# Building the in-pair table of an S5 scan during the scan itself, from a table turned back on TensorE, instead of in the front of the kernel

## The chip, the cores and the metric

The kernel runs on one NeuronCore of a Trainium2 chip. A core has TensorE (PE, with its weight loads listed apart as PEld), VectorE (DVE), ScalarE (ACT), GpSimd (POOL) and SyncE (SP), which here only issues DMA transfers. The metric is the device time of one execution in microseconds. The kernel before takes 2447.58 us (median of 3 runs, 2445.82 to 2447.65). The execution that the profiler recorded took 2450.09 us, with a span of 2448.3 us.

## What is computed

The program is a trunk of two residual layers on 256 tokens of width 2048. Layer 0 mixes tokens with a diagonal complex state-space model (S5), layer 1 with sparse attention; each is followed by a SwiGLU FFN, and shift, scale and gate of every sublayer come from a conditioning vector. The change lies in the S5 mixer:

```python
u = h @ in_w                                     # 128 groups of 16 channels
lam_bar = jnp.exp(lam * dt)
b_bar = ((lam_bar - 1.0) / lam)[..., None] * bmat
bu = jnp.einsum('gnp,blgp->lbgn', b_bar, ug)
# states[l] = lam_bar * states[l-1] + bu[l]
_, states = lax.associative_scan(combine, (a_seq, bu), axis=0)
y = jnp.real(jnp.einsum('gpn,lbgn->blgp', cmat, states)).reshape(Bsz, L, D)
y = y + d_skip.astype(f32) * u.astype(f32)
g = jax.nn.gelu(y).astype(h.dtype)
z = g @ glu_w + glu_b
```

Each group has 64 complex states. Everything is in float32.

## The kernel before

**Pairs of tokens.** The 256 tokens are taken in 128 pairs. VectorE runs the recurrence over pairs, so a step multiplies by the square of `lam_bar` and 128 states are made, not 256. What the first token of a pair gives to a state is in the table `Btab[1]` (B times lambda), what the second gives in `Btab[0]` (B). The output of a pair's second token needs the state before the pair, through C times lambda and so on, and also a term inside the pair: its own input through C times B, plus the skip term. `K0` holds that term, one 128 x 128 tile for each of the 16 blocks `f` of 128 channels, nonzero only inside groups of 16 channels. `Ddiag` holds the skip term alone, as 16 diagonal tiles, for the first token.

**The front (0 to 68 us).** TensorE and ScalarE turn C and B into tables. `turn_diag` (L1936) transposes `Bdiag` (B spread to block-diagonal form) into `Btab[0]`, four tiles at a time, with ScalarE copying the bank out (L868). `in_pair` (L1946) then multiplies `Bdiag` by `Ctab[0]`, 8 matmuls of 128 x 128 x 128 for each of 4 banks (L1952); VectorE multiplies each bank by a 0/1 mask into `K0` (`masked`, L1354). Later, in the first projection, VectorE adds the skip diagonal to `K0` in 16 instructions (`add_skip`, L1255). Between these, VectorE makes B times lambda in four big multiplications (`times_lam`, L1332), whose last one (L1346) must end before TensorE can transpose the imaginary half.

**Column units.** The conditioning vector is multiplied by `ada_w`, which streams from HBM in units of 512 KB through a ring of buffers `col_raw`. TensorE takes two units at a time with four matmuls (`col_units`, L1856; trace lines L1868 in the front, L1879 in the scan stage). I call that a pair of units. 64 units are consumed up to the end of the projection, and 64 more in the scan stage, through a ring of 7 buffers (`STATE_RING`): SyncE issues a unit's DMA as soon as TensorE has read the unit 7 places earlier.

**The projection (68 to 178 us)** takes 32 weight units of 512 KB, each rounded into a high part by ScalarE (L836) and a low part by VectorE (L1190), and 12 TensorE matmuls each (L2275). The other half of the column units is interleaved with its first 12.

**The scan stage (178 to 331 us).** TensorE's order is `s5()` (L2111): `inputs(0..7)` (L2058) fill the states; `outputs_inside(1, f)` and `outputs_inside(0, f)` (L2071 with `Ddiag`, L2072 with `K0`) with a pair of units after every second `f`; `outputs_inside(2, f)` with a pair after every `f`; four more pairs; then `outputs(0, f)` and `outputs(1, f)` (L2081), which need the first half of the scan, with the last nine pairs; then `outputs_inside(3)`, the first products of the GLU (L2093, L2107), `outputs(2)` and `outputs(3)`, which need the end of the scan. TensorE works strictly in that order. VectorE meanwhile runs 147 steps of the scan, six instructions each (L1531, L1536, L1542). At step 66 it reads the third row of column sums, which needs 32 of the 64 units.

## Time and profile before

| | |
|---|---|
| median of 3 runs | 2447.58 us |
| the profiled execution, and its span | 2450.09 us, 2448.3 us |
| TensorE busy, share of the span | 2395.8 us, 98% |
| VectorE, ScalarE busy | 1862.1 us (76%), 1039.9 us (42%) |
| bytes moved by DMA, mean rate | 630.53 MB, 258 GB/s |
| first matmul of the projection (L2275) | 67.68 us |
| last `inputs` matmul done, first `outputs(0)` matmul | 200.4 us, 257.1 us |
| last step of the scan | ends at 319.1 us |
| last `outputs(3)` matmul done | 331.4 us |

The profile is one execution. Times of rows count from the start of its span. A timeline or a chain of waits gives start and length in us; "x8" counts instruction records, of which an fp32 matmul leaves two. An idle time in brackets names what ended it. "PEclk" is the clock granted to TensorE, as a share of 2.4 GHz, so 1.00 and 0.50 are its two levels, 2.4 and 1.2 GHz. TensorE is busy nearly everywhere, so most of the 2448 us is its own work. The two places that the change touches are the front and the scan stage.

### The profile page before, as it was taken

How to read it: one execution, taken by the hardware profiler on the slowest of the kernel's cores; microseconds unless marked ns; L12 is line 12 of the kernel's file. 1: busy time of each engine (PE TensorE's matmuls, PEld its weight loads, DVE VectorE, ACT ScalarE, POOL GpSimd, SP SyncE). 2: the span in 40 equal slices, each digit the busy share in tenths (PEclk: the TensorE clock that was granted, in tenths of full speed). 3: DMA queues.
4: the chain of work that ended last, by engine and by line, in shares of the span. 5: the costliest groups of instructions: out<-in, count | busy, mean ns of one | idle time of the engine just before them, and what ended most of it. 6: DMA issues, size and time to landing. Idle time of an engine off the chain costs nothing.

```text
span 2448.3 us, 33308 instructions
## 1 busy us (share of the span) xinstructions
PE 2395.8 (98%) x12561; PEld 1918.2 (78%) x12561; DVE 1862.1 (76%) x3012; ACT 1039.9 (42%) x1241; POOL 35.3 (1%) x67
## 2 busy tenths in 40 slices
PE   7999899999999999999999999999999999999998
PEld 5585578778888888888878888778888888888886
DVE  8469979878888887888879987887777754455457
ACT  4353133464434444344454434555444344443442
POOL 0000000000000000000000000000000000000000
PEclk9997999999999999999999999999999999999999
DMA  9977959779889997898758877646788666656674
GB/s 373 399 256 278 373 169 328 234 236 349 306 284 308 342 308 259 292 339 297 256 162 291 284 254 226 201 141 192 253 300 279 220 196 189 189 190 191 194 223 139
DMA packets 313335, 630.53 MB, mean 258 GB/s; under 512 B 26740, under 2 KB 27156, under 8 KB 313176
## 3 DMA queue, kind: packets, MB, share of 16 engines
q1 hardware_dynamic: 307664, 613.36, 74.2%
q0 software_dynamic: 4288, 13.90, 2.0%
q8 instruction: 101, 1.65, 0.3%
q10 hardware_dynamic: 1224, 1.14, 0.1%
q14 instruction: 58, 0.48, 0.1%
HBM read 626.20 MB, written 2.11 MB: 257 GB/s over the span
## 4 chain that ended last, share of the span: by engine, by line
PE 90%; DVE 5%; issue 2%; DMA 2%; ACT 1%; SPq 0%; DVEq 0%; ACTq 0%
PE psB L2275 39%; PE psA L2275 39%; PE psT L1836 1%; PE psM L1868 1%; DMA col_raw<-in_ada_w 1%; PE psM L1879 1%; PE psB L2093 1%; DVE ada_acc L1207 1%; DVE w_lo L1190 1%; PE psT L2081 1%; PE psM L2107 1%; PE psT L2275 0%; PE psT L1900 0%; PE psA L2081 0%; PE psA L2058 0%
## 5 line engine op out<-in xcount | busy, mean ns | idle before, releaser
L1190 DVE TENSOR_TENSOR w_lo<-w_raw,w_hi 128x1024 fp32r<-128x1024 f32 x728 | 887.8, 1223 | 460.0 <-ACT w_hi L836 455.4
L836 ACT ACTIVATE w_hi<-w_raw 128x1024 fp32r<-128x1024 f32 x728 | 770.7, 1060 | 1093.5 <-PE psB L2275 486.6
L2275 PE MATMUL psB<-w_hi,hT_hi 128*128 128x512 f32 x1040 | 407.4, 392 | 0.0
L2275 PE MATMUL psB<-w_hi,hT_lo 128*128 128x512 f32 x1040 | 404.9, 389 | 0.0
L2275 PE MATMUL psB<-w_lo,hT_hi 128*128 128x512 f32 x1040 | 404.7, 389 | 0.0
L2275 PE MATMUL psA<-w_hi,hT_hi 128*128 128x512 f32 x1008 | 397.6, 394 | 2.3 <-DVE w_lo L1190 2.0
L2275 PE MATMUL psA<-w_hi,hT_lo 128*128 128x512 f32 x1008 | 392.8, 390 | 0.0
L2275 PE MATMUL psA<-w_lo,hT_hi 128*128 128x512 f32 x1008 | 392.5, 389 | 0.0
L1207 DVE SCALAR_TENSOR_TENSOR ada_acc<-ada_raw,csil,ada_acc 128x512 f32<-128x512 f32 x465 | 347.1, 746 | 14.6 <-DVE ada_acc L1207 0.5
L2275 PEld LDWEIGHTS psB<-w_hi,hT_hi 128*128 128x128 f32 x1040 | 195.3, 188 | 46.0 <-issue 4.5
L2275 PEld LDWEIGHTS psA<-w_hi,hT_hi 128*128 128x128 f32 x1008 | 189.2, 188 | 49.1 <-issue 8.0
L2275 PEld LDWEIGHTS psB<-w_hi,hT_lo 128*128 128x128 f32 x1040 | 195.2, 188 | 40.8
L2275 PEld LDWEIGHTS psB<-w_lo,hT_hi 128*128 128x128 f32 x1040 | 195.3, 188 | 39.8
L2275 PEld LDWEIGHTS psA<-w_hi,hT_lo 128*128 128x128 f32 x1008 | 189.2, 188 | 39.9
L2275 PEld LDWEIGHTS psA<-w_lo,hT_hi 128*128 128x128 f32 x1008 | 189.4, 188 | 37.8
L2275 PE MATMUL psA<-w_hi,aT_hi 128*128 128x512 f32 x448 | 175.3, 391 | 2.7 <-DVE w_lo L1190 1.9
L2275 PE MATMUL psA<-w_hi,aT_lo 128*128 128x512 f32 x448 | 174.4, 389 | 0.0
L2275 PE MATMUL psA<-w_lo,aT_hi 128*128 128x512 f32 x448 | 174.3, 389 | 0.0
L2275 PE MATMUL psB<-w_hi,aT_hi 128*128 128x512 f32 x400 | 156.3, 391 | 1.3 <-DVE w_lo L1190 1.3
L2275 PE MATMUL psB<-w_hi,aT_lo 128*128 128x512 f32 x400 | 155.7, 389 | 0.0
L2275 PE MATMUL psB<-w_lo,aT_hi 128*128 128x512 f32 x400 | 155.6, 389 | 0.0
L2275 PEld LDWEIGHTS psA<-w_hi,aT_hi 128*128 128x128 f32 x448 | 84.1, 188 | 21.5 <-DVE w_lo L1190 2.7
(399 smaller groups left out, 2356.7 us busy)
## 6 DMA issues: line engine op xcount, KB each, us to landing
w_raw<-in_ffn_w_in SPq DMA_DIRECT2D x352, 512.0 KB, 4.5
ada_raw<-in_ada_w SPq DMA_DIRECT2D x496, 256.0 KB, 5.3
w_raw<-in_ffn_w_out SPq DMA_DIRECT2D x176, 512.0 KB, 4.7
col_raw<-in_ada_w SPq DMA_DIRECT2D x128, 512.0 KB, 7.3
w_raw<-in_dsa_in_w SPq DMA_DIRECT2D x112, 512.0 KB, 4.7
w_raw<-in_s_glu_w SPq DMA_DIRECT2D x56, 512.0 KB, 5.5
w_raw<-in_s_in_w SPq DMA_DIRECT2D x32, 512.0 KB, 8.1
w_raw<-in_dsa_out_w SPq DMA_DIRECT2D x32, 512.0 KB, 4.9
```

The source lines that it names most:

```text
L836: nc.scalar.activation(high(u), w_raw[:, u % RING], ACT.Copy).then_inc(w_hi_ready, 1)
L1190: V.tensor_tensor(low(u), w_raw[:, u % RING], high(u).bitcast(F32), ALU.subtract).then_inc(w_lo_ready, 1)
L1207: V.scalar_tensor_tensor(out=ada_sum(q), in0=ada_tile(q, k), scalar=csil[:, k:k + 1], in1=ada_sum(q), op0=ALU.mult, op1=ALU.add).then_inc( ...
L1836: ins = nc.tensor.transpose(T[:, j // 2, (j % 2) * SEQ + t * P:(j % 2) * SEQ + (t + 1) * P], src(t, j), ident[:])
L1868: ins = MM(M[row:row + 32, 0], csil[:, k:k + 1].to_broadcast([P, 32]), col_tile(a + w)[:, b * NB:(b + 1) * NB], start=k == 0, stop=k == AU ...
L1879: ins = MM(M[row:row + 32, v % 2], csil[:, k:k + 1].to_broadcast([P, 32]), col_tile(a + half)[:, b * NB:(b + 1) * NB], start=k == 0, stop= ...
L2081: ins = MM(outputs_place(n, f, d)[rows], Ctab[d][ri][:, f, rows], st[:, c0:c0 + HALF, half, g, ri, f % 8], start=False, stop=f % 4 == 3 an ...
L2093: ins = MM(gated_bank(0, t), uT[:, kt, tok], glu_raw[k][:, kk], start=kt == 0, stop=kt == KT - 1)
L2107: ins = MM(gated_bank(1, 0), uT[:, kt, 0:P], raw[:, kk], start=kt == 0, stop=kt == KT - 1)
L2275: ins = MM(PS[s][:, t, 0:r.width] if into is None else into, a_[:, kt, tok], b_[:, kk, 0:r.width], start=kt == begin and m == 0, stop=kt = ...
```

## The change

The in-pair term is no longer made in the front. `in_pair` with its 32 matmuls, `masked` and `add_skip` are gone, and so are the waits on them. GpSimd clears `K0` at the start. In the scan stage, after the last `inputs`, TensorE transposes the 32 tiles of `Btab[0]` back into state-major form (`turn_back`, 8 banks of 4 tiles), ScalarE copies each bank to `Bback` (over `Btab[1]`, no longer needed then), and TensorE multiplies `Bback` by `Ctab[0]` in 128 matmuls that write 32 x 32 blocks of one PSUM bank. Four matmuls of an identity block by `Ddiag` add the skip term, and ScalarE copies the four diagonal strips to `K0` in four instructions. Only then may `outputs_inside` start. The pairs of units are placed anew: four among the eight `turn_back`, one behind the new `in_pair`, and in the third group one after every second `f` in place of every `f`.

```diff
+        Bback = [at(f"Bback_{ri}", "aT_lo", [P, KT, P], plus=ri * 8 * K) for ri in range(2)]
...
                 elif col_slot(a)[0] == CRING:
-                    sp.wait_ge(pair_full, 4)
                     sp.wait_ge(scaled_ready, 2)
...
+            nc.gpsimd.memset(K0[:], 0.0).then_inc(pair_zeroed, 1)
...
+                for n in range(8):
+                    act.wait_ge(back_turned, n + 1)
+                    nc.scalar.activation(Bback[n // 4][:, 4 * (n % 4):4 * (n % 4) + 4, :],
+                                         PS[0][:, n % 2].rearrange("p (j m) -> p j m", m=P), ACT.Copy).then_inc(back_stored, 1)
+                act.wait_ge(pair_full, 1)
+                act.wait_ge(pair_zeroed, 1)
+                for g in range(4):
+                    rows = slice(32 * g, 32 * g + 32)
+                    nc.scalar.activation(K0[rows, :, rows], PS[0][rows, 0].rearrange("p (f m) -> p f m", m=32), ACT.Copy
+                                         ).then_inc(pair_stored, 1)
...
-            def add_skip(f):
-
-                V.scalar_tensor_tensor(out=K0[:, f], in0=ident[:], scalar=dcol[:, f:f + 1], in1=K0[:, f], op0=ALU.mult, op1=ALU.add
-                                       ).then_inc(pair_skipped, 1)
...
-            for n in range(3):
-                col_units(20 + 2 * n, 22 + 2 * n)
-                in_pair(n)
-            col_units(26, 30)
-            in_pair(3)
-            col_units(30, VUNITS)
+            col_units(20, VUNITS)
...
+            def turn_back(n):
+
+                if n >= 2:
+                    pe.wait_ge(back_stored, n - 1)
+                for k in range(4):
+                    ins = nc.tensor.transpose(PS[0][:, n % 2, k * P:(k + 1) * P], Btab[0][n // 4][:, 4 * (n % 4) + k, :], ident[:])
+                ins.then_inc(back_turned, 1)
+
+            def in_pair():
+
+                pe.wait_ge(back_stored, 8)
+                for f in range(KT):
+                    for ri in range(2):
+                        for g in range(4):
+                            rows = slice(32 * g, 32 * g + 32)
+                            MM(PS[0][rows, 0, 32 * f:32 * f + 32], Bback[ri][:, f, rows], Ctab[0][ri][:, f, rows],
+                               start=f + ri == 0, stop=False)
+                pe.wait_ge(diag_ready, 2)
+                for g in range(4):
+                    rows = slice(32 * g, 32 * g + 32)
+                    ins = MM(PS[0][rows, 0].rearrange("p (f m) -> p f m", m=32), ident[rows, rows], Ddiag[rows, :, rows],
+                             start=False, stop=True, tile_position=(32 * g, 32 * g))
+                ins.then_inc(pair_full, 1)
...
-                pe.wait_ge(diag_ready, 2)
-                pe.wait_ge(pair_skipped, KT)
+                pe.wait_ge(bu_read_act, 22)
+                for n in range(8):
+                    turn_back(n)
+                    if n % 2:
+                        units(2)
+                in_pair()
+                units(2)
+                pe.wait_ge(pair_stored, 4)
                 for half, read in ((1, 20), (0, 24)):
...
                 for f in range(8):
                     outputs_inside(2, f)
-                    units(2)
-                units(8)
+                    if f % 2:
+                        units(2)
+                units(6)
```

TensorE in the front of the kernel before, from the fifth pair of column units before the end of that stretch (`col_raw` is a ring buffer of units, `C0_0_tab` the real half of `Ctab[0]`):

```order
L1868 MATMUL psM<-col_raw2_72,csil_96 32x512 x4
L1952 MATMUL psA<-C0_0_tab_123,Bdiag_re_141 128x128
L1952 MATMUL psA<-C0_1_tab_124,Bdiag_im_142 128x128
L1952 MATMUL psA<-C0_0_tab_123,Bdiag_re_141 128x128
L1952 MATMUL psA<-C0_1_tab_124,Bdiag_im_142 128x128
```

The same place in the changed kernel, up to the first transposes of B times lambda:

```order
L1861 MATMUL psM<-col_raw_72,csil 32x512 x4
L1861 MATMUL psM<-col_raw_73,csil 32x512 x4
L1861 MATMUL psM<-col_raw_74,csil 32x512 x4
L1861 MATMUL psM<-col_raw_75,csil 32x512 x4
L1861 MATMUL psM<-col_raw_71,csil 32x512 x4
L1861 MATMUL psM<-col_raw_72,csil 32x512 x4
L1935 MATMUL psA<-ident,BLdiag_re 128x128 x4
```

The four blocks of eight matmuls between the pairs of units are gone, and the six pairs now follow one another.

TensorE in the scan stage of the kernel before, behind the last `inputs`:

```order
L2058 MATMUL psB<-uT_105,B1_1_tab_122 128x127 x2
L2071 MATMUL psT<-uT_105,Ddiag_83 128x64
L2072 MATMUL psT<-uT_105,K0_127 128x64
L2071 MATMUL psT<-uT_105,Ddiag_83 128x64
L2072 MATMUL psT<-uT_105,K0_127 128x64
L1879 MATMUL psM<-col_raw2_72,csil_96 32x512 x2
```

And in the changed kernel (L2077 are the transposes of `turn_back`, L1872 the units, L2087 the small in-pair matmuls, of which 32 such rows follow):

```order
L2034 MATMUL psB<-uT,B_1_tab 128x127 x2
L2077 MATMUL psA<-ident,B_0_tab 128x128 x8
L1872 MATMUL psM<-col_raw_72,csil 32x512 x2
L1872 MATMUL psM<-col_raw_70,csil 32x512 x2
L2077 MATMUL psA<-ident,B_0_tab 128x128 x8
L1872 MATMUL psM<-col_raw_70,csil 32x512 x4
L2077 MATMUL psA<-ident,B_1_tab 128x128 x8
L1872 MATMUL psM<-col_raw_70,csil 32x512 x2
L1872 MATMUL psM<-col_raw_71,csil 32x512 x2
L2077 MATMUL psA<-ident,B_1_tab 128x128 x8
```

```order
L2087 MATMUL psA<-C_1_tab,Bback_129 32x32 x4
L2092 MATMUL psA<-Ddiag,ident 32x512 x4
L1872 MATMUL psM<-col_raw_70,csil 32x512 x4
L2047 MATMUL psT<-uT,Ddiag 128x64
L2048 MATMUL psT<-uT,K_127 128x64
L2047 MATMUL psT<-uT,Ddiag 128x64
```

Thirty-two transposes, 128 small matmuls and 4 wide ones now stand between the last `inputs` and the first `outputs_inside`, with five pairs of units among them; the pairs behind are fewer by as many.

## Rows read from the trace of the kernel before

**Rows 1.** The page: TensorE's busy time, and its granted clock in 40 slices.

```profile
PE 2395.8 (98%) x12561; PEld 1918.2 (78%) x12561; DVE 1862.1 (76%) x3012; ACT 1039.9 (42%) x1241; POOL 35.3 (1%) x67
PEclk9997999999999999999999999999999999999999
```

**Rows 2.** Stretches: length, busy us (instructions) of each engine, PEclk, DMA share, GB/s.

```profile
10.00:60.00 50.00, 47.17 (x500) 30.50 (x501) 43.27 (x56) 26.04 (x46) 0.00 (x0) 1.00 1.03 404
60.00:116.00 56.00, 54.51 (x308) 33.23 (x307) 27.18 (x40) 22.82 (x29) 0.00 (x0) 1.00 1.03 401
209.10:236.20 27.10, 27.10 (x116) 12.61 (x120) 27.10 (x173) 0.00 (x0) 0.00 (x0) 0.50 0.92 321
283.60:331.40 47.80, 47.75 (x613) 30.53 (x614) 40.05 (x258) 5.85 (x6) 0.00 (x0) 1.00 0.55 195
```

**Rows 3.** Chain of waits in the front: start, length, what.

```profile
46.24 1.98 PE psA L1952 x16
58.01 0.99 PE psM L1868 x8
61.02 2.20 DVE BLdiag_im L1346
```

**Rows 4.** VectorE in the front, a `masked`; and all of `add_skip`, grouped.

```profile
51.23 0.69 DVE L1357 TENSOR_TENSOR K<-psB,cst 128x512 f32<-128x512 f32 x1
L1257 DVE SCALAR_TENSOR_TENSOR K<-ident,dcol,K 128x128 f32<-128x128 f32 x16 | 4.8, 344 | 0.0
```

**Rows 5.** Last pair of units of the front: its two DMAs, and their time to landing.

```profile
L630 SPq DMA_DIRECT2D col_raw<-in_ada_w x2: 327/380/432, 46.3 to 46.6; - x2
DMA to landing us min/median/max: 6.8/7.3/7.8
```

**Rows 6.** Last pair of the projection: its DMAs, landing, and (chain) its matmuls.

```profile
L630 SPq DMA_DIRECT2D col_raw<-in_ada_w x2: 328/380/431, 104.8 to 105.2; - x2
DMA to landing us min/median/max: 9.4/9.9/10.3
116.48 0.99 PE psM L1868 x8
```

**Rows 7.** ScalarE and VectorE behind the last `inputs`: scan step 20 starts.

```profile
200.50 1.12 ACT L1025 ACTIVATE st<-psA 128x512 f32<-128x512 f32 x2 [1.25 <-PE psB L2058]
202.63 0.49 DVE L1531 TENSOR_TENSOR prod<-st,lam 128x128 f32<-128x128 f32 x2 [0.64 <-ACT st L1025]
```

**Rows 8.** TensorE in the scan stage, pairs of units; the first two at full clock.

```profile
203.44 1.06 PE L1879 MATMUL psM<-col_raw,csil 128*32 128x512 f32 x8
205.47 1.06 PE L1879 MATMUL psM<-col_raw,csil 128*32 128x512 f32 x8
209.08 1.83 PE L1879 MATMUL psM<-col_raw,csil 128*32 128x512 f32 x8 [1.51 <-DMA col_raw<-in_ada_w]
216.50 1.94 PE L1879 MATMUL psM<-col_raw,csil 128*32 128x512 f32 x8
220.27 1.94 PE L1879 MATMUL psM<-col_raw,csil 128*32 128x512 f32 x8
255.54 1.78 PE L1879 MATMUL psM<-col_raw,csil 128*32 128x512 f32 x8 [0.62 <-DMA col_raw<-in_ada_w]
```

**Rows 9.** Four transposes of `turn_diag` on TensorE; a bank copied by ScalarE.

```profile
59.00 0.59 PE psA L1942 x4
40.39 0.59 ACT L868 ACTIVATE B_tab<-psB 128x512 f32<-128x512 f32 x1
```

**Rows 10.** Chain of waits at the end of the stage: `outputs(2)`, `outputs(3)`.

```profile
313.24 7.26 PE psA L2081 x226
324.13 5.88 PE psT L2081 x181
```

**Rows 11.** The column unit issued at 222.2 us: time to landing.

```profile
DMA to landing us min/median/max: 3.6/3.6/3.6
```

**Rows 12.** VectorE: the last steps of the scan.

```profile
318.84 0.31 DVE L1542 TENSOR_TENSOR st<-tmp,st 128x32 f32<-128x32 f32 x2
```

More of the change, by code:

```diff
@@ L290, in build @@
         gate_saved = sem("gate_saved")
-        pair_skipped = sem("pair_skipped")
         glub_landed, sigmoid_done = sem("glub_landed"), sem("sigmoid_done")
@@ L306, in build @@
         imag_turned, imag_stored = sem("imag_turned"), sem("imag_stored")
-        pair_full, pair_masked, c_scaled = sem("pair_full"), sem("pair_masked"), sem("c_scaled")
+        c_scaled, pair_zeroed, back_turned, back_stored = sem("c_scaled"), sem("pair_zeroed"), sem("back_turned"), sem("back_stored")
+        pair_full, pair_stored = sem("pair_full"), sem("pair_stored")
         part_free, part_added = [sem("part_free0"), sem("part_free1")], sem("part_added")
@@ L930, in _ @@
             make_h(0)
-            act.wait_ge(pair_full, 4)
             h_high(0)
@@ L1353, in _, with row_at_last @@
             vec.wait_ge(c_scaled, 2)
-            def masked(n):
-                vec.wait_ge(pair_full, n + 1)
-                V.tensor_tensor(K0[:, 4 * n:4 * n + 4], PS[n % 2][:, n // 2 % 2].rearrange("p (j m) -> p j m", m=P),
-                                cst[:, 98:98 + P].unsqueeze(1).to_broadcast([P, 4, P]), ALU.mult).then_inc(pair_masked, 1)
-            def masked_then_row(n):
-                masked(n)
+            def row_at_last(n):
                 if n == 3:
@@ L1373, in _ @@
             vec.wait_ge(bdiag_ready, 8)
-            times_lam(pairs(BLdiag[0], True), pairs(BLdiag[1], True), [pairs(b, True) for b in Bdiag], True, scaled_ready, masked_then_row)
+            times_lam(pairs(BLdiag[0], True), pairs(BLdiag[1], True), [pairs(b, True) for b in Bdiag], True, scaled_ready, row_at_last)
             vec.wait_ge(scaled_turned, 2)
@@ L1780, in _ @@
                         lo_to(n, 2, filled_to(r))
-                        if n == 2:
-                            vec.wait_ge(pair_masked, 4)
-                        if 2 <= n < 10:
-                            add_skip(2 * n - 4)
-                            add_skip(2 * n - 3)
                         if n in (14, 16):
@@ L1944, in turn_diag @@
                 ins.then_inc(full, 1)
-            def in_pair(n):
-                pe.wait_ge(b_stored, n + 5)
-                for k in range(4):
-                    f = 4 * n + k
-                    for ri in range(2):
-                        ins = MM(PS[n % 2][:, n // 2 % 2, k * P:(k + 1) * P],
-                                 Bdiag[ri][:, 4 * f:4 * f + 4].rearrange("p g a k -> p (g a k)"), Ctab[0][ri][:, f],
-                                 start=k + ri == 0, stop=k + ri == 4)
-                ins.then_inc(pair_full, 1)
             pe.wait_ge(act_prep, 3)
@@ L1982, in _ @@
                 turn_diag(n, Bdiag, bdiag_ready, 5, b_stored, b_turned)
-            for n in range(3):
-                col_units(20 + 2 * n, 22 + 2 * n)
-                in_pair(n)
-            col_units(26, 30)
-            in_pair(3)
-            col_units(30, VUNITS)
+            col_units(20, VUNITS)
             pe.wait_ge(scaled_ready, 1)
             for n in range(2):
-                turn_diag(n, BLdiag, pair_masked, 1, scaled_stored, scaled_turned)
+                turn_diag(n, BLdiag, b_stored, 5, scaled_stored, scaled_turned)
             turn_row(0, M[:, 1], front_row[:, 0])
-            turn_diag(2, BLdiag, pair_masked, 1, scaled_stored, scaled_turned)
+            turn_diag(2, BLdiag, b_stored, 5, scaled_stored, scaled_turned)
             pe.wait_ge(lam_spread, 1)
@@ L1997, in _ @@
             for n in range(4, 7):
-                turn_diag(n, BLdiag, pair_masked, 1, scaled_stored, imag_turned)
-            turn_diag(3, BLdiag, pair_masked, 1, scaled_stored, scaled_turned)
+                turn_diag(n, BLdiag, b_stored, 5, scaled_stored, imag_turned)
+            turn_diag(3, BLdiag, b_stored, 5, scaled_stored, scaled_turned)
             pe.wait_ge(cols_added, 2)
@@ L2010, in projection @@
                 r = s5_in
-                pe.wait_ge(pair_masked, 4)
                 pe.wait_ge(scaled_stored, 3)
```

## The prediction

> **What bounds the kernel now.** I read four views, in this order. The page first: TensorE is busy 98% of the span, and its granted clock is below full in one slice of forty, the one from 184 to 245 us, which is the scan stage [rows 1]. So time is won where TensorE waits or is slow, and any work added to it costs its own length unless it fills a wait. Second, the stretches [rows 2]: from 10 to 116 us the DMA engines are saturated, 404 and 401 GB/s, at a DMA share over 1. A unit of 512 KB then takes 524,288 B / 404 GB/s = 1.30 us, and a pair 2.6 us. From 209.1 to 236.2 us TensorE is busy all the time at a granted clock of 0.50 while DMA moves only 321 GB/s; from 283.6 to 331.4 us it is busy 47.75 of 47.80 us. Third, the chain of waits: in the front it runs on TensorE and VectorE [rows 3], at the end of the scan stage on TensorE through `outputs(2)` and `outputs(3)` [rows 10]. Fourth, VectorE's timeline, which ends the scan at 318.84 + 0.31 = 319.1 us [rows 12], 5.0 us before TensorE starts `outputs(3)` at 324.13 [rows 10]. The scan stage is therefore bound by TensorE's order and by the column units in it, not by the recurrence: whatever delays TensorE between 200 and 283 us shifts the end one for one, and the most that speeding it up can bring is 5.0 us, for then the recurrence is last.
>
> **The front: what is removed.** Four blocks of `in_pair` take 1.98 us each, 7.9 us of TensorE on the chain [rows 3]. Four `masked` of 0.69 us and 16 `add_skip` leave VectorE, 2.8 and 4.8 us [rows 4]. What is late next? The last pair of units of the front is issued at 46.3 and 46.6 us, just when TensorE is through with the pair that frees their buffers and the first `in_pair` begins, 46.24 [rows 3]; so the change doesn't move it. It lands 7.8 us after 46.6, at 54.4 [rows 5]. TensorE reads it at 58.01 now [rows 3]; it can't before 54.4. So the front gains 58.0 - 54.4 = 3.6 us, not 7.9. VectorE's L1346 at 61.02 [rows 3] hangs on the row that is turned after this pair and moves with it.
>
> In the projection the saturated DMA takes the rest. The last pair of units there is issued at 104.8 and 105.2, lands at 105.2 + 10.3 = 115.5, and is used at 116.48 [rows 6]: 0.95 us of slack. Since DMA runs at 401 GB/s throughout [rows 2] and its queue holds the same transfers in the same order, that landing stays. TensorE arrives up to 3.6 us early and waits until 115.5. The front is worth **0.9 us**, bounded by 0, if the landing slips as far, and 3.6, if landings follow TensorE. VectorE's saving is worth nothing: TensorE runs on through the stretch while VectorE is busy 27 of 56 us [rows 2]. GpSimd's extra memset lies at the start, where it has nothing else. All of the scan stage shifts by the 0.9 us; below I keep the old time axis and subtract it at the end.
>
> **The scan stage: what is added.** From 200.4 us on, where the last `inputs` end and ScalarE starts on their bank at 200.50 [rows 7]:
> - The wait for ScalarE's copy of the bank: 200.50 + 1.12 = 201.6 [rows 7].
> - Eight times four transposes at 0.59 us [rows 9], 4.7 us, and four pairs of units at 1.0 [rows 8]: 201.6 + 4.7 + 4.0 = 210.3 us. ScalarE's eight copies at 0.59 [rows 9] run beside the pairs.
> - 128 small matmuls. The nearest row is `outputs(2)`: 128 matmuls with weights of the same form and twice the columns take 7.26 us [rows 10], 57 ns each. I take 7.3 us; half of it, 3.6, if the time goes by columns, and 14.6 if it doubles at half clock. To 217.6.
> - Four identity matmuls of 512 columns, like the four of a pair, 0.9 us: 218.5.
> - A pair of units beside ScalarE's four copies into `K0`; the rows show none of 32 partitions. At a bank copy's 0.59, pipelined at about 0.5, they take 2.1 us (bounds 1.2 and 2.4). `outputs_inside` starts at 220.6.
>
> At 200.4 us it started before, so 20.2 us of TensorE time stand in front of it, of which five pairs (5 us) are only moved: 15 us are new. What pays for them is that TensorE waits for units later, and what decides how much is the clock.
>
> **At full clock.** Two `f` and a pair take 205.47 - 203.44 = 2.03 us [rows 8]. Twelve such turns and three pairs end at 220.6 + 24.4 + 3.0 = 248.0, but the units are not there. All seven buffers of the ring are full during the small matmuls, so DMA stands still; the first buffer comes free at 219.5, with pair 8, and a lone unit needs 3.6 us [rows 11], 223.1. The second unit of pair 23, the last before `outputs(0)`, is 24 units later: 223.1 + 24 x 1.30 = 254.3. `outputs(0)` starts at 255.3. Before, it started at 257.1, behind a pair 23 that had waited for DMA until 255.54 [rows 8]: a gain of 1.8.
>
> **At half clock.** The clock fell to 0.50 in the turn in which TensorE had waited 1.51 us for a unit, at 209.08 [rows 8], and although TensorE was then busy without a gap it stayed there 27 us [rows 2]. A turn of two `f` and a pair takes 220.27 - 216.50 = 3.77 us in it [rows 8]. What followed was a third group with a pair after every `f`; only in it did the clock return, and the change removes that denser pattern. In the changed kernel the stretch behind 201.6 is made of short transposes with handshakes and of small 32-column matmuls with half the columns of any before. I expect the clock to fall in or just before the small matmuls, and to stay through about six turns: 220.6 + 6 x 3.77 = 243.2 us. By then 28 units of 64 are used and the next two freed buffers fill at 246.8 and 248.1; the last unit of pair 23 is 11 later, 262.4, and `outputs(0)` starts at 263.4: **6.3 us late**. With five turns, which is nearer to the 27 us measured, it is 5.2; if all twelve turns are low, 220.6 + 45.2 + 1.9 + 2.0 = 269.7, 12.6 us late.
>
> One rule speaks here. "TensorE: Matmul & The Clock Gate" of the Trainium skill, in its section on the HAM clock gate, says that the throttled state is the default, that sustained matmul activity releases it and that idle gaps bring it back. By that rule the new block, which puts TensorE to work where it had waited, would keep the clock up, and the sum would be the one at full clock. This trace speaks against taking it so simply: 27.1 busy us of 27.1 at 0.50 [rows 2].
>
> The scan stays hidden. Step 66 starts at 202.63 + 46 x 0.94 = 245.9 (173 instructions in 27.1 us, six a step [rows 2, 7]); the pair it needs is ready at about 249, so VectorE stalls some 3 us, and ends at 322 against an `outputs(3)` that moves to 330.
>
> **The sum.** Against the profiled execution's 2450.09 us: -0.9 (front) + 6.3 (scan stage) = +5.4, so 2455.5. That execution was 2.5 us above the median 2447.58; for the median I forecast **2453.0 us**.
>
> **The rivals.**
> - *The clock holds (B).* The rule above, and the fact that the one wait of 1.51 us may vanish, speak for it; the 27 busy us at 0.50 against. -0.9 - 1.8 = -2.7: 2444.9 us. The same kernel as before, to what can be measured.
> - *The units stream freely (C).* The clock holds and the small matmuls cost 3.6 us. "TensorE: Matmul & The Clock Gate", section on the back-to-back issue gap, gives about 25 ns as the least distance of two matmuls; 128 of them would take 3.2 us by it, and the estimate would be C's. The trace's 57 ns for wider ones with the same weights [rows 10] is against. Then -0.9 - 5.5, stopped by the end of the recurrence at -0.9 - 5.0 = -5.9: 2441.7 us.
> - *Low clock to the end (A2).* The forecast's mechanism at its full length, from the small matmuls to the three pairs: -0.9 + 12.6 = +11.7: 2459.3 us. For it: nothing in that stretch resembles what ended the low clock before. It decides as soon as the clock fails to return by 243 us.
> - *The small matmuls double (D).* They take 14.6 us at half clock: 7.3 more on A or A2, 2460 to 2467 us. The trace shows matmuls of this form at full clock alone, so this can't be excluded.
> - *The front gives what it removes (E).* If units landed earlier once TensorE frees the buffers earlier, the front would bring up to 3.6 us, and every case would be 2.7 lower. Against it: 401 GB/s at a DMA share of 1.03 [rows 2].
>
> **How the numbers follow.** A difference under 0.2%, 4.9 us, is what a measurement of this kernel can't tell from no change. Forecast with five to eight low turns: 0.31. A2: 0.20; D 0.05; B 0.31; C 0.13. E is spread over them as a shift. Faster by over 4.9 us holds C, less a part that stays inside, and E with B: 0.12. Slower by over 4.9: A2, D and somewhat more than half of the forecast's case: 0.43. Within: 0.45. The range that leaves out a tenth at each side runs from between B and C to A2: 2443 to 2460.5 us. The forecast's own range is 2450 to 2457.
>
> **What would show it.** Right: the pair of units at 58.01 moves to 54.4, and the one at 116.48 to 115.5 behind an idle TensorE ended by DMA; the first projection matmul comes 3.6 us earlier, the first `inputs` 0.9; the small matmuls take 7 us; a window from 215 to 243 us shows 0.50; `outputs(0)` starts at 262; the recurrence ends before `outputs(3)` begins. Wrong: a PEclk of 1.00 from 200 to 250 us (B or C), a scan stage that begins over 2 us earlier (E), or small matmuls far from 7.3 us.

## The result and the profile after

| | before | changed |
|---|---|---|
| median (runs) | 2447.54 us (10) | 2455.14 us (10) |
| lowest to highest | 2445.82 to 2449.03 | 2453.91 to 2472.53 |
| profiled execution, span | 2450.09, 2448.3 | 2469.1, 2467.4 |

The ratio is 1.005, 95% interval 1.0036 to 1.0063: slower by 0.4 to 0.6%, where 2453.0 us was forecast, 1.002 of before. The changed kernel's times don't scatter evenly: six lie at 2453.9 to 2455.2, one at 2458.0, three at 2469.1 to 2472.5. The profiled execution is one of the three. A second profile of the same kernel is of an execution of 2456.3 us, near the median; both are shown.

The page of the changed kernel, 2469.1 us: busy times, and the granted clock in 40 slices [rows 1].

```profile
PE 2406.8 (98%) x12793; PEld 1924.5 (78%) x12793; DVE 1856.1 (75%) x2992; ACT 1046.6 (42%) x1253; POOL 37.0 (1%) x68
PEclk9997899999999999999999999999999999999999
```

TensorE is busy 11 us longer, in a span 19.1 us longer, and the dip in slices 4 and 5 (185 to 308 us) lasts longer. Where is the time? `outputs(0)` started at 257.1 before and starts at 273.1 now; `outputs(3)` at 324.1 and 342.4; what follows is the same work. The end of the scan stage in the chain of waits [rows 10]:

```profile
331.49 7.25 PE psA L2057 x225
342.37 7.23 PE psT L2057 x228
```

So 16.0 of the 19 us arise before `outputs(0)`. About 0.5 of them are there before the new block: the last `inputs` are done at 201.0 us, before at 200.4. The stretches that answer to [rows 2], in the same columns, first of the 2469.1 us execution:

```profile
10.00:60.00 50.00, 43.42 (x449) 25.41 (x450) 41.89 (x58) 27.79 (x49) 0.00 (x0) 0.93 1.03 404
60.00:116.00 56.00, 53.00 (x294) 31.67 (x292) 22.18 (x20) 21.29 (x27) 0.00 (x0) 1.00 1.03 402
215.80:270.20 54.40, 52.40 (x293) 25.93 (x297) 49.65 (x313) 7.34 (x7) 0.00 (x0) 0.50 0.75 249
```

and of the 2456.3 us execution:

```profile
216.00:223.00 7.00, 4.89 (x89) 1.49 (x89) 7.00 (x47) 1.70 (x3) 0.00 (x0) 0.53 0.34 136
223.00:254.00 31.00, 25.06 (x196) 13.73 (x192) 30.78 (x193) 5.64 (x5) 0.00 (x0) 1.00 0.98 374
254.00:264.50 10.50, 8.18 (x96) 3.04 (x100) 10.50 (x68) 0.00 (x0) 0.00 (x0) 0.51 1.03 408
```

The same program has its half clock for 54 us in one execution, and in the other for 7 and again for 10 us, with 31 us at full clock between them (and for some 3 us more at 203 to 206 us, before these stretches). In the full-clock stretch TensorE is busy 25 of 31 us and DMA runs at a share of 0.98: there the column units are the bound, not TensorE.

TensorE's timeline through the new block in the 2469.1 us execution (start, length, group, and in brackets the idle time before it and its releaser):

```profile
209.25 1.06 PE L1872 MATMUL psM<-col_raw,csil 128*32 128x512 f32 x8
210.13 1.78 PE L2087 MATMUL psA<-C_tab,Bback 128*32 128x32 f32 x183
216.53 1.22 PE L2087 MATMUL psA<-C_tab,Bback 128*32 128x32 f32 x73 [4.62 <-issue]
217.68 1.93 PE L2092 MATMUL psA<-Ddiag,ident 32*32 32x512 f32 x8
222.15 0.69 PE L2047 MATMUL psT<-uT,Ddiag 128*128 128x64 f32 x2 [0.68 <-ACT K L1034]
```

The small matmuls are 1.78 us of work, a hole of 4.62 us that no engine's work releases, and 1.22 us of work, now at half clock. What the hole is comes out below, in the experiment with the matmuls doubled.

Two of the pairs of units behind it, one turn of two `f` and a pair apart, at half clock:

```profile
227.82 1.94 PE L1872 MATMUL psM<-col_raw,csil 128*32 128x512 f32 x8
231.59 1.94 PE L1872 MATMUL psM<-col_raw,csil 128*32 128x512 f32 x8
```

### The profile page after: what moved, and what is told of

Read it like the earlier page. It is cut to its first block, busy times and chain, and to the rows that moved or that the text cites. A ratio compares the mean times of both kernels' runs of the same rounds, so it can differ in the third digit from the quotient of the medians.

```text
span 2467.4 us, 33763 instructions
## 1 busy us (share of the span) xinstructions
PE 2406.8 (98%) x12793; PEld 1924.5 (78%) x12793; DVE 1856.1 (75%) x2992; ACT 1046.6 (42%) x1253; POOL 37.0 (1%) x68
## 4 chain that ended last, share of the span: by engine, by line
PE 89%; DVE 5%; issue 3%; DMA 2%; ACT 1%; SPq 0%; DVEq 0%; ACTq 0%
PE psB L2282 39%; PE psA L2282 38%; PE psM L1872 2%; DVE ada_acc L1217 1%; PE psT L1829 1%; PE psB L2069 1%; PE psM L1861 1%; DVE w_lo L1200 1%; DMA col_raw<-in_ada_w 1%; PE psT L2057 1%; PE psM L2107 1%; DMA w_raw<-in_s_in_w 0%; PE psT L1893 0%; PE psA L2034 0%; PE psA L2057 0%
## 5 line engine op out<-in xcount | busy, mean ns | idle before, releaser
L1217 DVE SCALAR_TENSOR_TENSOR ada_acc<-ada_raw,csil,ada_acc 128x512 f32<-128x512 f32 x465 | 347.5, 747 | 14.6 <-DVE ada_acc L1214 0.5
```

The costliest lines, as they stand in the source:

```text
L1217: V.scalar_tensor_tensor(out=ada_sum(q), in0=ada_tile(q, k), scalar=csil[:, k:k + 1], in1=ada_sum(q), op0=ALU.mult, op1=ALU.add).then_inc( ...
```

## The experiments

Twelve kernels ran beside the kernel before. Each row's profile is of one execution, and the ratios below refer to runs of the kernel before from the same hour. In the table "low" is the time at half clock between 200 and 286 us, worked out from stretches of 2 us as (1 - PEclk) x 2 x 2 us.

| kernel | all runs, us (median) | profiled | low | `outputs(0)` |
|---|---|---|---|---|
| before | 2444.2 to 2455.6 (2446.6 to 2447.5) | 2450.1 | 37.6 | 257.1 |
| changed | 2453.9 to 2472.5 (2455.1) | 2469.1 | 54.6 | 273.1 |
| changed, again | 2454.2 to 2460.0 (2456.4) | 2456.3 | 20.5 | 261.9 |
| front alone | 2445.1 to 2448.6 (2446.9) | 2446.2 | 20.5 | 251.3 |
| scan alone | 2469.5 to 2470.8 (2470.2) | 2470.0 | 54.6 | 272.2 |
| no small matmuls | 2457.6 to 2462.3 (2461.5) | 2457.6 | 37.6 | 260.8 |
| slices | 2445.7 to 2464.4 (2449.5) | 2445.9 | 0.0 | 253.0 |
| dense third group | 2457.1 to 2469.6 (2465.5) | 2469.6 | 51.2 | 275.0 |
| three pairs behind | 2452.0 to 2466.1 (2460.3) | 2459.6 | 34.1 | 266.6 |
| wide matmuls | 2452.8 to 2467.4 (2457.4) | 2453.4 | 10.3 | 259.9 |
| slices, large extra | 2463.8 to 2474.0 (2468.5) | 2463.8 | 0.0 | 270.6 |
| before, large extra | 2450.2 to 2455.7 (2453.8) | 2454.8 | 10.2 | 261.5 |
| doubled | 2463.7 to 2476.7 (2466.3) | 2463.7 | 23.9 | 269.4 |
| slices, small extra | 2451.1 to 2455.9 (2452.8) | 2451.1 | 0.0 | 256.3 |

**The changed kernel again.**

> The changed kernel itself, for its spread and for a second profile. Its ten runs so far lie at 2454 to 2455 (six), 2458 (one) and 2469 to 2473 (three), with mean granted clocks of 0.993 to 0.995, 0.992 and 0.985. Theory (the clock sets the mode): a profile near 2454 shows the low clock of the scan stage ending before about 245 us and outputs(0) near 262, and one at 2469 shows it up to 270 us. Rival (the mode is set somewhere else, as in the front or in the rest of the kernel): both profiles have the same scan stage, and the 15 us lie before 200 or after 350 us.

Measured: 2456.4 us, ratio to before 1.0038 [1.0025, 1.0052]. The theory holds in that the scan stage sets the mode: `outputs(0)` at 261.9 against 273.1, and the last `inputs` are done at 200.9 and 201.0 us, so nothing before differs. It fails on the course: the low clock isn't one stretch to 245 us but three, the first of them during the transposes, at 203 to 206 us, behind a wait of 1.20 us for ScalarE. The other execution has the same wait, 1.21 us, and no fall there.

**The front alone.** Change: the block in the scan stage and its copies are taken out, and the units stand as before. The kernel leaves out the in-pair term.

```
-                for n in range(8):
-                    turn_back(n)
-                    if n % 2:
-                        units(2)
-                in_pair()
-                units(2)
-                pe.wait_ge(pair_stored, 4)
+                pe.wait_ge(diag_ready, 2)
+                pe.wait_ge(pair_zeroed, 1)
```

> The front half of the change alone: in_pair, masked and add_skip are gone and K0 is only cleared, so the in-pair table is left out of the result; units placed as in the kernel before. Theory (the projection's DMA is saturated and takes the front's gain back): 0.9 us faster than before, 2446.5, first inputs 0.9 earlier, last pair of the front at 54.4. Rival (landings follow TensorE): 3.6 faster, 2444. Second rival, from the profile of the changed kernel, where TensorE ran at half clock after waiting 8 us for that pair: the gain is eaten by the clock, 0 us, and the first inputs come no earlier.

Measured: 2446.92 us against 2446.87, ratio 0.9996 [0.9987, 1.0005]. A gain of 3.6 us (0.15%) lies outside the interval; 0.9 and 0 can't be told apart. The chain of waits of the changed kernel shows where the gain ends:

```profile
92.55 10.27 DMA w_raw<-in_s_in_w
102.84 0.03 ACT w_hi L837
103.80 1.01 ACT partial L1141
104.86 3.03 PE psB L2282 x12
116.65 0.99 PE psM L1861 x8
```

Before, TensorE ran through this point with the same 12 matmuls at 104.7 us; now it is there earlier and waits 1.44 us for ScalarE, which stands behind a weight unit that lands at 102.8. The pair of units at the end comes at 116.65, before at 116.48 [rows 6]. In the front itself the waits, 1.49, 1.50 and 0.62 us before three pairs, cost extra:

```profile
46.45 8.05 DMA col_raw<-in_ada_w
54.64 1.94 PE psM L1861 x8
```

The pair lands where forecast, and then runs at half clock: 1.94 us, not 0.99 [rows 3]. The kernel with slices, below, has the same front; behind waits of 1.28, 1.49 and 1.51 us its clock held there:

```profile
63.37 2.75 PE psA L2284 x12
88.63 13.24 DMA w_raw<-in_s_in_w
```

Its first matmul of the projection comes at 63.4 us, 4.3 earlier than before, its wait at the same weight unit is 2.13 us in place of 1.44, and its last pair comes at 115.7. So it is the weight unit that takes the gain, with or without the clock. What is left can't be read from single profiles: the last `inputs` are done at 199.6, 200.4 and 202.2 us in the three kernels with the old front, and between 200.1 and 202.3 in those with the new one.

**The scan half alone.** Change: the kernel before with its front, plus the block in the scan stage, which overwrites K0 with the same values; units as in the changed kernel.

> The scan half of the change alone: the front still builds the table as before, and the scan stage builds it again and overwrites it. Theory (the scan stage is the cost, and adds to the front): about 0.9 slower than the changed kernel, 2455.9, modes included. Rival (the slow mode of the changed kernel comes from the front, where an idle stretch lets the clock fall): no slow mode here, all runs near 2455 to 2456. If the changed kernel's cost came from the front after all: 2447.5.

Measured: 2470.2 us, four runs from 2469.5 to 2470.8, 1.0093 [1.0079, 1.0107]. Both numbers were wrong: neither 2455.9 nor 2455 to 2456. The rival is refuted, since the slow mode comes without the change in the front; here it came every time. The block and the low clock behind it are enough for the whole cost.

**No small matmuls.**

```
-                for f in range(KT):
-                    for ri in range(2):
-                        for g in range(4):
-                            rows = slice(32 * g, 32 * g + 32)
-                            MM(PS[0][rows, 0, 32 * f:32 * f + 32], ...)
```

> The changed kernel without the 128 small matmuls, so the products of the in-pair table are left out and only the skip term is in it. In the changed kernel's profile they take 7.55 us, of which 4.62 is a stall of TensorE that nothing in the profile releases, and the clock is at 0.50 behind it. Theory (that stall brings the clock down): the clock holds at 1.00 through the stage, outputs(0) at about 254, and the time is 2445 to 2446. Rival (the clock falls anyway, by the short transposes with their handshakes): the low stretch of 25 us or more stays, the 7.5 us are the only gain of TensorE, and the time is 2449 to 2452.

Measured: 2461.5 us, slower than with them. My theory of that moment is refuted: the hole isn't needed for the fall. The clock held through the block, to the first long wait for a column unit, and fell there:

```profile
221.78 0.39 PE L2048 MATMUL psT<-uT,K 128*128 128x64 f32 x2
222.00 0.38 PE L2047 MATMUL psT<-uT,Ddiag 128*128 128x64 f32 x2
222.23 0.38 PE L2048 MATMUL psT<-uT,K 128*128 128x64 f32 x2
224.32 1.78 PE L1872 MATMUL psM<-col_raw,csil 128*32 128x512 f32 x8 [1.71 <-DMA col_raw<-in_ada_w]
```

It came back at 258 us, in three pairs of units in a row. The kernel leaves out the products, but keeps the skip term. What this and the other profiles bear out: every fall between 200 and 286 us lies in an idle stretch of TensorE or within 2 us behind one, the shortest of 1.2 us, whatever caused it. The reverse doesn't hold. Here a wait of 1.39 us for `K0` at 215.2 took nothing down, nor did 1.68 and 1.55 us in the kernel with slices. How long the clock stays down goes with what stands behind the fall.

**Slices.** The small matmuls in four parts with a pair of units behind each.

```
-                in_pair()
-                units(2)
+                for f in range(0, KT, 4):
+                    in_pair(f, f + 4)
+                    units(2)
```

> The changed kernel with its 128 small matmuls in four slices of 32, a pair of column units behind each, and nothing behind the third group (same pairs in all). Theory (TensorE is held in the small matmuls because 256 records pass faster than its instructions arrive, and the pairs between them give that time back): the stalls without a releaser, 4.6 us in one piece, go or fall under 1 us in sum, the clock doesn't fall there, and the time is 2449 to 2451. Rival (the stall hangs on something else, such as a place in the program that moves with the instructions): 4 to 5 us of stall stay, somewhere in the slices, and the time is that of the changed kernel, 2454 to 2456.

Measured: 2449.5 us median, 1.0021 [1.0004, 1.0038], eight of twelve runs at 2445.7 to 2451.8 and four at 2459.9 to 2464.4. Profiled was one of 2445.9 us with the clock at 1.00 all the way. Of the hole of 4.6 us 0.96 is left, in the third slice:

```profile
214.40 1.06 PE L1872 MATMUL psM<-col_raw,csil 128*32 128x512 f32 x8 [1.68 <-DMA col_raw<-in_ada_w]
215.25 0.59 PE L2087 MATMUL psA<-C_tab,Bback 128*32 128x32 f32 x38
216.81 0.44 PE L2087 MATMUL psA<-C_tab,Bback 128*32 128x32 f32 x26 [0.96 <-issue]
```

The mechanism of the theory is supported (its "under 1 us" too); its time is met by the median only, since runs near 2462 remain. With the clock held, little of the block's cost shows: `outputs(0)` starts at 253.0, 1.7 us later than in the front alone, and that execution takes what the kernel before takes, though the kernel before has 37.6 us of half clock in its own profile. The slices also bring three pairs of units from behind the third group ahead of it; the experiment with three pairs behind the block does that alone, and it is slower, so the gain isn't from there.

**Dense third group.** A pair of units behind each f there, as in the kernel before.

> The changed kernel with a pair of column units behind every f of the third group, as in the kernel before; one of the four pairs among the transposes and the three behind the group are gone for it. Theory (at half clock a turn of two f and a pair is too thin to bring the clock back, a turn of one f and a pair brings it back): a low stretch that reaches the third group ends in it, as at 236 in the kernel before, so runs of 2469 turn into about 2459 and the median is 2453 to 2456, no run above 2462. Rival (how long the clock stays low has nothing to do with the pattern): runs near 2469 as often as in the changed kernel.

Measured: 2465.5 us, four of six runs above 2462. The bound on the runs is refuted, but the pattern does what was said. TensorE's timeline at the seam, where eight turns of two f and a pair have just run at half clock:

```profile
254.60 1.94 PE L1872 MATMUL psM<-col_raw,csil 128*32 128x512 f32 x8
257.52 1.33 PE L1872 MATMUL psM<-col_raw,csil 128*32 128x512 f32 x8
259.36 1.07 PE L1872 MATMUL psM<-col_raw,csil 128*32 128x512 f32 x8
```

The clock is back in the second dense turn. What I missed is that by then the eight thin turns have cost their time, and at full clock the dense turns wait for DMA, so that it falls again at 269 us. In all profiles of the table a clock that was low in a turn of two f and a pair stayed low to the last such turn: twelve in the changed kernel and in the scan half alone, eight here and without the small matmuls, five with three pairs behind. It came back in dense turns or in pairs in a row, and in one place (at about 206 us, five profiles) among the transposes and the pairs between them.

**Three pairs behind.** Three pairs behind the new `in_pair` instead of one.

> The changed kernel with three pairs of column units behind the new in_pair instead of one, and one instead of three behind the third group. All seven buffers are full there, so the three pairs are 5.8 us of wide matmuls at half clock without a wait. Theory (wide matmuls in a row bring the clock back): the clock is back at 1.00 before the first outputs_inside in every profile, no run near 2469, median 2452 to 2454. Rival (it comes back by chance): some runs near 2469, and the others 2454 to 2456.

Measured: 2460.3 us, runs from 2452.0 to 2466.1. In the profile the clock is back within the three pairs, as expected:

```profile
220.03 1.93 PE L2092 MATMUL psA<-Ddiag,ident 32*32 32x512 f32 x8
221.89 3.38 PE L1872 MATMUL psM<-col_raw,csil 128*32 128x512 f32 x24
```

But the ring is then empty, a wait of 1.62 us for DMA ends at 241.8, and the clock falls at about 243.6 and stays down for 24 us, thin turns again. "No run near 2469" holds, for six runs with the highest at 2466.1; the time doesn't.

**Wide matmuls.** The product as 32 matmuls of 128 x 128 and 4 of 128 x 512, with 16 copies by ScalarE.

> The changed kernel with the in-pair product as 32 matmuls of 128 x 128 and 4 of 128 x 512 for the skip term, in four banks, and 16 copies into K0 by ScalarE in place of 4; pairs of units behind the second and the fourth bank. At full clock 4 x (1.98 + 0.25) = 8.9 us of TensorE, against 7.55 + 0.97 with the 4.6 us stall in it. Theory (the stall lets the clock fall and the low clock is the cost): no stall, no fall before the first wait for DMA, and 2449 to 2452. Rival (the added TensorE time is the cost, whatever the clock): as the changed kernel or slower, 2455 to 2458.

Measured: 2457.4 us, 1.0046 [1.0030, 1.0062]: inconclusive between the two. The profile (2453.4 us) shows no hole and the clock at 1.00 from 208 to 250 us, as the theory has it; it also has a fall that the theory excludes, at 203 us in the transposes. The block takes 12.0 us with a pair in it, where 8.9 and 1.0 were counted, and `outputs_inside` starts at 225.2:

```profile
211.93 2.05 PE L2093 MATMUL psA<-C_tab,Bback 128*128 128x128 f32 x16
213.81 1.02 PE L2094 MATMUL psA<-Ddiag,ident 128*128 128x512 f32 x2
```

A matmul of 128 x 512 with all 128 columns of weights takes 0.87 to 0.97 us; I had counted 0.25.

**Slices with large extra matmuls.**

```
+                for _ in range(n):
+                    MM(PS[0][:, 1]..., ident[:], Ddiag[:, 0:4], start=True, stop=True)
```

> The kernel with slices plus 30 extra matmuls of 128 x 512 (0.24 us each at full clock, 7.1 us in all) whose results nobody reads: two behind each slice, four before the wait for K0, two in each turn of two f and a pair, up to the middle of the third group. At full clock they lie in time in which TensorE waits for DMA, since a turn takes 2.03 us and a pair of units 2.6. Theory (idle stretches let the clock fall, and turns of two f and a pair are too thin to bring it back; that alone separates the 2446 and 2463 of the kernel with slices): more work for TensorE makes it faster, all runs between 2445 and 2450, median 2447. Rival (the falls are not tied to what TensorE does): runs at 2460 and above as often as without them, the median 2449 or more, and every low stretch longer by 0.5 us a turn.

Measured: 2468.5 us. The wrong price of the wide matmuls again, now decisive: the 0.24 us that I took from a pair of units belongs to matmuls of 32 weight columns, four of which run side by side. An extra one takes 0.93, and a turn 3.80 us at full clock, as long as at half clock without them.

```profile
229.59 1.93 PE L2116 MATMUL psA<-Ddiag,ident 128*128 128x512 f32 x4
231.45 1.06 PE L1872 MATMUL psM<-col_raw,csil 128*32 128x512 f32 x8
```

The time says nothing on the theory; the clock does. It is 1.00 from 200 to 276 us.

**The kernel before with large extra matmuls.**

> The kernel before plus such extra matmuls: two in each turn of two f and a pair of the first two groups but the first turn, one behind each of the first four f of the third. Theory: its low stretch of 27 us goes too, but the recurrence ends at 319 us whatever TensorE does, so it gains only what the executions above that bound lose: median 2446, against 2447.2, and no run above 2449. Rival (the kernel before isn't near any bound in the scan stage, and the low clock costs it its full 10 us or so): 2440 or less.

Measured: 2453.8 us, 1.0023 [1.0014, 1.0032], the price error once more (`outputs(0)` at 261.5, 4.4 late, in an execution whose last `inputs` were 1.7 late already). The 27 us at half clock are gone; 10 us remain at 251 to 261, where no extra matmul stands and TensorE waits for units. The claim on 2446 us is not tested by it.

**Doubled.** The 128 small matmuls issued twice.

> The changed kernel with the 128 small matmuls issued twice, the second time over the first. Read from the profile's stretch of them, not from the time. Theory (their pace, 256 records in 7.55 us, is that at which instructions reach TensorE; the 9.7 ns a record in the first burst is what was waiting in a queue): the stretch is about 15 us, one burst of some 180 records and then stalls that nothing in the profile releases, 10 us or more in sum. Rival (a single stall of 4.6 us tied to one place): 7.55 + 2.5 = 10 us, with one stall.

```profile
211.73 1.78 PE L2088 MATMUL psA<-C_tab,Bback 128*32 128x32 f32 x183
218.73 1.93 PE L2088 MATMUL psA<-C_tab,Bback 128*32 128x32 f32 x128 [5.22 <-issue]
222.46 1.93 PE L2088 MATMUL psA<-C_tab,Bback 128*32 128x32 f32 x128 [1.79 <-issue]
225.92 1.22 PE L2088 MATMUL psA<-C_tab,Bback 128*32 128x32 f32 x73 [1.52 <-issue]
```

512 records take 15.3 us, twice 7.6, with 8.5 us of holes, under the 10 or more expected. The theory holds in the rest, and the single hole is refuted: behind a first burst the records come in portions of 128, every 3.5 to 3.7 us, though TensorE needs 1.9 for a portion even at half clock. The kernel took 2466.3 us.

The DMA queue that carries instructions shows what the portions are. Its lines in three stretches of 0.1 or 0.2 us, from 216.2, 219.8 and 223.5 us (transfers, MB, share):

```profile
q8 instruction: 1, 0.02, 29.6%
q8 instruction: 1, 0.02, 73.5%
q8 instruction: 1, 0.02, 59.9%
```

Each is one transfer of 16 KB. The trace has them from 216.29 to 217.24, 219.86 to 221.04 and 223.57 to 224.53 us, and TensorE goes on at 218.73, 222.46 and 225.92: 1.4 to 1.5 us behind the end of each. In the changed kernel such a transfer ends at 215.02, and its hole at 216.53. The holes of over 1 us put down to "issue" behind 260 us fit too: in the changed kernel they end at 281.37, 294.50 and 300.91, and transfers end 1.3 us before each; in the kernel before one ends at 281.67, 1.35 us behind a transfer.

**Slices with small extra matmuls.** A quarter of the size, 0.23 us by the row above.

> The kernel with slices plus extra matmuls of 128 x 128, a quarter of the size of the extra ones tried before, which took 0.93 us each: three behind each slice, five before the wait for K0, two in each turn of two f and a pair up to the middle of the third group. By that row they take 0.23 us each at full clock, and a turn 2.03 + 0.47 = 2.5 us, still under the 2.6 in which a pair of units lands. Theory (falls come from idle stretches, and the low clock alone separates the 2446 and 2463 of the kernel with slices): no run above 2452, median 2446 to 2448. Rival (such short matmuls don't count against a fall, or the falls have another cause): runs at 2460 and above remain, in about a third of them, as without the extra matmuls.

Measured: 2452.8 us, 1.0025 [1.0015, 1.0034], ten runs within 2451.1 to 2455.9, the clock at 1.00 throughout. A turn is 2.53 us:

```profile
229.88 0.66 PE L2116 MATMUL psA<-Ddiag,ident 128*128 128x128 f32 x4
230.47 1.06 PE L1872 MATMUL psM<-col_raw,csil 128*32 128x512 f32 x8
233.00 1.06 PE L1872 MATMUL psM<-col_raw,csil 128*32 128x512 f32 x8
```

The first half of the theory is supported: with TensorE less idle none of ten runs falls into the 2460s, where four of twelve did (if the extra matmuls changed nothing, that would come about by chance 7 times in 100). Idle stretches remain, of 0.67 and 1.52 us in the block, and the clock held. The bound of 2452 us and the median aren't met: `outputs_inside` starts at 226.5, where slices had 222.9, and `outputs(0)` at 256.3 instead of 253.0. A version that keeps the clock by extra work pays about what it saves.

None of these beats the kernel before. The front alone equals it, but leaves out the in-pair term. The best that computes it all, slices, beats the changed kernel by about 6 us and lies 0.2% above before.

## Why the prediction was right, and where it wasn't

**The front: nothing against 0.9 us, and nothing that shows it.** The pair at 58.01 [rows 3] starts at 54.64, forecast 54.4. The front alone measured 0.04% (1.0 us) faster, between 3.2 faster and 1.2 slower, forecast 0.9; the rival that it gives 3.6 (E) is just excluded, and 0 isn't. Three steps weren't as told. "The first projection matmul comes 3.6 us earlier": it came 1.35 earlier, because the clock had fallen to 0.50 in the front, behind the waits for units. The gain ends at 104.9 us, at a weight unit, not at the pair of 116.5, which comes at 116.65 and not at 115.5: the first thing that a saturated queue delivers late stops the gain. And the last `inputs` are 0.5 us later than before, not 0.9 earlier, in both profiles of the changed kernel, within the spread of single profiles.

**The block's length: right, with a wrong reason.** Forecast 7.3 us for the small matmuls, measured 7.55. I took 57 ns each from `outputs(2)` [rows 10], as if TensorE worked so long. It works 19 ns each (183 records in 1.78 us) and for the rest waits for its instructions. That the price came out is luck as far as is known: 256 records take 7.3 us in `outputs(2)` without a gap, and 7.55 here with one of 4.62. Rival C's 3.6 us and D's 14.6 are both refuted by the rows. `outputs_inside` began at 222.15 and 223.7, forecast 220.6 - 0.9 = 219.7.

**The low clock: this step failed.** It was the heart of the forecast: about six turns at 3.77 us, 215 to 243 us at 0.50. The turn was exact (3.77), the count was not. One profile has all twelve turns low, the other none. The count was taken from one stretch of 27 us in one profile of the kernel before. That same profile has a second low stretch, from about 247 to 257 us, which the prediction doesn't mention:

```profile
252.98 1.94 PE L1879 MATMUL psM<-col_raw,csil 128*32 128x512 f32 x8 [0.62 <-DMA col_raw<-in_ada_w]
```

The execution with twelve low turns is rival A2. It was priced at 11.7 us over before and measured 19.0: 4.3 of the missing 7.3 lie before `outputs(0)` (273.1 for 268.8; a start at 222.2 instead of 219.7, and waits of 0.59 and 1.25 us for units behind the turns), 3.0 behind it, where holes of 1.0, 1.7 and 1.4 us for instructions stand (before: one of 1.2).

**The sum: right by a different addition, so in part by luck.** In the execution of 2456.3 us `outputs(0)` starts at 261.87, forecast 262.5. But the turns there ran at full clock, the last eight paced by DMA at 2.5 to 2.6 us each, so the sum is the one that I had for the full clock: first freed buffer, 24 units, and a pair. The buffer came free at 222.1, not 218.6 (219.5 - 0.9), because the small matmuls began at 211.65, 2.3 us later than forecast, and the rest of the block ran at half clock; from 216 to 223 us the DMA moved only 136 GB/s. Then 222.1 + 3.6 + 31.2 = 256.9; the last pair came at 260.2, behind waits of 2.04, 0.62 and 1.35 us with the clock at 0.50 again:

```profile
254.34 1.94 PE L1872 MATMUL psM<-col_raw,csil 128*32 128x512 f32 x8 [2.04 <-DMA col_raw<-in_ada_w]
260.19 1.94 PE L1872 MATMUL psM<-col_raw,csil 128*32 128x512 f32 x8 [1.35 <-DMA col_raw<-in_ada_w]
```

So B's mechanism was at work, at another price, and the 6.3 us that I gave to the half clock are in the typical execution mostly DMA that stood still or was late.

**The recurrence as the bound: not refuted, not shown.** It ended at 324.6 us in the changed kernel, before `outputs(3)` at 342.4, as forecast. Where the stage goes well the two come close: `outputs(3)` starts at 319.9 in the kernel with slices and the scan ends at 319.5; in the front alone 319.4 and 319.0.

```profile
319.21 0.31 DVE L1540 TENSOR_TENSOR st<-tmp,st 128x32 f32<-128x32 f32 x2
319.88 7.30 PE L2057 MATMUL psT<-st,C_tab 128*32 128x64 f32 x256
```

That is 4.2 and 4.6 us earlier than before, where the cap is 5.0. But TensorE has no gap before `outputs(3)` in any profile, so it is nowhere seen to wait for the recurrence. None of the twelve kernels had a run under 2445.0 us, and the lowest of before is 2444.2, which agrees with a bound and doesn't prove it.

**The clock and the rule.** The rows show the clock falling behind waits, and returning most often in wide matmuls in a row. "TensorE: Matmul & The Clock Gate" of the Trainium skill, in its section on HAM oscillation, says that waits for DMA between bursts of matmuls throttle the clock again and again; the falls at 224 us without the small matmuls (behind 1.71 us) and at 254 us in the changed kernel (behind 2.04) agree, and the 1.68 us in the kernel with slices, without a fall, show that not each wait does it. Its section on the HAM clock gate has sustained activity release it; 54.4 us at 0.50 with TensorE busy in 52.4 of them say that being busy wasn't enough here: it didn't return in twelve turns of two `f` and a pair. Taken as simply as the prediction put it for its rival B, that the new block would keep the clock up, the rule fails in both profiles of the changed kernel.

**What stays open.** The low stretch that begins in the block ended at 223 us in one execution and not in the other, though the same 3.8 us of wide matmuls stood in both, 1.6 us later in the one in which it ended. Why the scan half alone hit the long mode four times of four, and the changed kernel three times of fifteen, isn't settled; only four runs stand behind the former. Three of ten and none of five runs in the long mode also say little on how often it comes. That TensorE is stopped by the delivery of instructions rests on the portions and on the times of the transfers; why a transfer starts when it does isn't shown. That the low clock alone separates the slices' runs near 2447 and near 2462 isn't shown either: none of the latter was profiled, though their mean clocks are lower, 0.986 to 0.989 against 0.994 to 0.999.

## What to carry to other kernels

Moving work out of a stretch that waits for a saturated DMA gained nothing that could be measured, so price such a move by its destination. Where a stage runs near the edge of the clock, count what a new idle stretch does to everything behind it: at half clock this pattern costs 3.77 us a turn in place of 2.6, for as long as the thin pattern lasts. Small matmuls are best put in portions among long ones, which hid nearly all of 4.6 us here.

## What the runs showed of the hardware that I had not expected

- Short matmuls in great number are bound by their instructions: 128 of 128 x 32 take 7.55 us and 256 take 15.3, with 128 records every 3.5 to 3.7 us, each portion 1.4 to 1.5 us behind a transfer of 16 KB on the instruction queue; TensorE needs 1.8 us for the first 183 records at full clock.
- A matmul of 512 fp32 columns takes 0.93 us with 128 columns of weights, while four with 32 columns each take 1.0 together.
- The same program got 20 us of half clock in the scan stage in an execution of 2456 us, and 54 in one of 2469.
